# Casting the next panel's weights ahead of the head squares in the first unit of a query or key panel

## The reference: what is computed

```python
h = _rmsnorm(x, g_mix)
z = h @ w_in
u, va, q, k, v, gate_a, gate_b = jnp.split(z, cuts, axis=-1)
u = jax.nn.gelu(u)
va = _rmsnorm(jax.nn.gelu(va), g_v)
a = mix_a(u, va, w_s, b_s)
q = _rotary(_rmsnorm(q.reshape(*lead, N_HEADS_B, HEAD_DIM), g_q), pos)
k = _rotary(_rmsnorm(k.reshape(*lead, N_HEADS_B, HEAD_DIM), g_k), pos)
v = v.reshape(*lead, N_HEADS_B, HEAD_DIM)
b, kv_states = mix_b(q, k, v)
merged = jax.nn.sigmoid(gate_a) * (a @ w_oa) + jax.nn.sigmoid(gate_b) * (b @ w_ob)
x = x + merged @ w_o
```

## Time and profile before

| | us |
|---|---|
| Median of 3 runs | 1079.61 |
| Lowest, highest | 1078.57, 1081.40 |
| The profiled execution | 1077.97 |
| Its span, first to last instruction | 1076.3 |

### The profile page before, as it was taken

The page is one execution under the profiler, slowest core; times in us unless marked ns, Lnnn a source line. Parts: engine busy times, 40 slices in busy tenths (PEclk is TensorE's granted clock), DMA queues, the critical chain, the costliest instruction groups (busy, mean ns, idle before and its releaser), DMA issues.

```text
span 1076.3 us, 21532 instructions
## 1 busy us (share of the span) xinstructions
PE 1043.8 (97%) x8507; PEld 1030.8 (96%) x8508; DVE 690.3 (64%) x881; ACT 484.1 (45%) x1181; POOL 242.7 (23%) x374
## 2 busy tenths in 40 slices
PE   8999999999987999999999999999999999999996
PEld 8999999999987998999999999999999999999996
DVE  5579888988887778999583354344434443445552
ACT  6772888569634664352264543123312321333331
POOL 2441334014210014949101210010001000102300
PEclk9999999999998999999999999999999999999999
DMA  6557565776797564777732345555555555555512
GB/s 199 197 174 233 189 199 177 258 223 209 218 264 234 177 199 146 220 202 209 244 117 77 106 144 196 166 186 191 194 168 184 191 197 174 182 188 166 165 41 83
DMA packets 131090, 196.20 MB, mean 182 GB/s; under 512 B 32208, under 2 KB 108272, under 8 KB 129216
## 3 DMA queue, kind: packets, MB, share of 16 engines
q1 hardware_dynamic: 105808, 122.46, 35.9%
q0 software_dynamic: 10304, 63.28, 18.6%
q10 hardware_dynamic: 14896, 9.34, 2.9%
HBM read 186.07 MB, written 62.00 MB: 230 GB/s over the span
## 4 chain that ended last, share of the span: by engine, by line
PE 67%; DVE 13%; ACT 6%; issue 5%; DMA 4%; SPq 4%; ACTq 1%; POOL 0%; DVEq 0%; POOLq 0%
PE gm L1112 53%; PE gm L1088 3%; PE gm L1089 3%; PE gm L1090 3%; DMA w_raw<-in_w_in 2%; DVE w_lo L1391 2%; ACT prob L953 2%; DVE kv L1553 2%; DVE kv L1512 1%; DVE acc L1559 1%; SPq L587 1%; ACT sq L663 1%; SPq L539 1%; ACT w_hi L644 1%; ACTq L968 1%
## 5 line engine op out<-in xcount | busy, mean ns | idle before, releaser
L1112 PE MATMUL gm<-h_hi,w_hi 128*128 128x272 f32 x1088 | 227.8, 291 | 0.3 <-issue 0.3
L1112 PE MATMUL gm<-h_hi,w_lo 128*128 128x272 f32 x1088 | 225.1, 288 | 0.0
L1112 PE MATMUL gm<-h_lo,w_hi 128*128 128x272 f32 x1088 | 224.3, 288 | 0.0
L644 ACT CAST w_hi<-w_raw 128x1024 fp32r<-128x1024 f32 x150 | 150.5, 1044 | 157.9 <-PE gm L1112 116.5
L1391 DVE TENSOR_TENSOR w_lo<-w_raw,w_hi 128x1024 fp32r<-128x1024 f32 x150 | 178.2, 1227 | 40.2 <-ACT w_hi L644 38.0
L1088 PE MATMUL gm<-w_hi,h_hi 128*128 128x256 f32 x640 | 187.3, 293 | 4.6 <-issue 4.4
L1089 PE MATMUL gm<-w_hi,h_lo 128*128 128x256 f32 x640 | 181.1, 283 | 0.0
L1090 PE MATMUL gm<-w_lo,h_hi 128*128 128x256 f32 x640 | 180.3, 282 | 0.0
L1112 PEld LDWEIGHTS gm<-h_hi,w_hi 128*128 128x128 f32 x1088 | 170.5, 188 | 1.1 <-issue 0.5
L1112 PEld LDWEIGHTS gm<-h_lo,w_hi 128*128 128x128 f32 x1088 | 171.0, 189 | 0.0
L1112 PEld LDWEIGHTS gm<-h_hi,w_lo 128*128 128x128 f32 x1088 | 169.9, 189 | 0.0
(11 more groups left out here) (263 smaller groups left out, 1531.3 us busy)
## 6 DMA issues: line engine op xcount, KB each, us to landing
w_raw<-in_w_ff SPq DMA_DIRECT2D x64, 512.0 KB, 5.1
out_kvs<-in_cache_kv_w POOLq DMA_DIRECT2D x64, 510.0 KB, 4.3
w_raw<-in_w_in SPq DMA_DIRECT2D x60, 512.0 KB, 6.4
kv<-in_cache_kv_w SPq DMA_DIRECT2D x128, 128.0 KB
kv<-in_cache_kv_w SPq DMA_DIRECT2D x64, 256.0 KB
out_kvs<-in_cache_kv_w POOLq DMA_DIRECT2D x32, 508.0 KB, 4.8
kv<-in_cache_kv_w POOLq DMA_DIRECT2D x128, 64.0 KB, 3.5
w_raw<-in_w_o SPq DMA_DIRECT2D x8, 512.0 KB, 4.8
```

Of the source, the lines that this page charges most:

```text
L644: nc.scalar.copy(w_hi[:, r, hh * 1024:(hh + 1) * 1024], w_raw[:, hh]).then_inc(w_hi_done, 1)
L1112: last = nc.tensor.matmul(gm[:, 2 * b2 + half, 0:HALF], w, x[:, k0 + k, half * HALF:(half + 1) * HALF], start=first, stop=end)
```

## The change

For q, k and va panels, the two casts of the next panel's weights are issued inside `evacuate`, right behind the copy of the first unit, and therefore ahead of the squares of q and k. For v and oa panels they stay behind `evacuate`. The instructions and their waits are the same.

```diff
                         nc.scalar.copy(z[:, r, 0:n], src).then_inc(unit_out, 1)
+                        if sub == 0:
+                            split_hi(p + 1, (p + 1) % 2, panel_end(p - 1) if p >= 1 else None)
                         if kind != "va":
                             act.wait_ge(unit_out, u + 1)
                             square_heads(u, slice(0, 128), slice(0, 128), z[:, r], 8, r)
...
                 evacuate(s)
-                if late_split(s):
+                if late_split(s) and kind in ("v", "oa"):
                     split_hi(p + 1, (p + 1) % 2, panel_end(p - 1) if p >= 1 else None)
```

## The result

The changed kernel takes 1083.27 us (median of 11 runs, 1079.65 to 1086.11) against 1079.61 us (11 runs, 1075.88 to 1081.65) of the kernel before: ratio 1.0036, 95% interval 1.0022 to 1.0049. In microseconds that is 3.7, where the prediction had 2.8; the time predicted was 1082.4 us. The loss is real, and its middle lies just beyond the 0.3% that the prediction had set as its limit for no change. The profiled execution took 1083.2 us (span 1081.6 us), 5.2 us more than the one of before, which was itself a quick one. 0.54 us of that lie ahead of the start of panel 1 (31.79 against 31.25) and are not the change's: the granted clock of the first 16 us was 0.89 in it and 1.00 in before, and of all 14 executions traced the four with 0.89 there begin panel 1 0.54 to 0.75 us later, the others within 0.13 us of before.

What follows compares the result with a forecast made beforehand. TensorE, busy 97%, was taken as the bound; 0.4 us (panel 6) + 0.5 us (panel 9) + 1.93 us (panel 12) made 2.8 us, put on the median 1079.61 us: 1082.4 us, +0.26%, range 1078.0 to 1086.0 us.

Steps and rivals of the forecast that it cites:

- What bounds the kernel: TensorE, busy 97% of 1076.3 us; a change helps only by shortening its waits and hurts by making one longer.
- The earlier cast brings nothing: Panels 0 to 2: split weights end about 1 us earlier, but TensorE has no wait there; bounds 0 to 2.9 us, taken 0.
- Panel 12: Squares stand behind late weights, so 1.93 us falls on all that follows; TensorE's transposes near 227 wait 1.5 to 2 us.
- Panel 9: GpSimd's root falls into VectorE's subtractions and delays `scale_heads`: 0 to 0.95 us, taken 0.5 us.
- Panel 6: Squares wait for weights landing at about 109.7, exponential 0.75 us later; 0.4 us taken for the loop of ScalarE and VectorE.
- No link with slack over 0.3 us: From `scale_heads` at 233.79 to TensorE's wait ending at 339.27, lag on the loop reaches the end of the program.
- Behind 340 everything shifts alike: After the long wait ending at 339.27 the order is unchanged, so all later work moves by the same lag.
- slower by weights that land later: Rival, chance 0.30: panel 12's second half lands later than 224.6, moving squares and transposes equally; 1083.4 to 1085.4 us.
- Swallowed: Rival, chance 0.11: SyncE's queue sets the landing at 337.0, so TensorE's wait ending at 339.27 absorbs the loss; 1079.6 us.
- Faster: Rival, chance 0.12: earlier casts free `w_raw` earlier, shrinking VectorE's backlog and panel-start waits; 1077.1 us, or 1074.2 us.
- panel starts 7, 13, 15, 16 without a wait: Sign that the forecast is wrong: TensorE no longer idle at the starts of these panels.

Runs made afterwards that it cites:

- The table of four: Lag at panel 16, panel 12's order against its weights: old late 0, new late +2.28 us, new with weights early -0.97 us, old with weights early not run.
- the table of landings: Ten full-load kernels: panel 12's second-half landing against lag growth to panel 16; the new order adds 1.87 to 1.99 us to the landing.
- only 6: New order of casts and squares in panel 6 alone, against the kernel before: 1079.43 against 1080.41 us, ratio 0.9983.
- the change with loads ahead: Whole change, with four loads of V put behind panel 13's weights in SyncE's queue, against the kernel before: 1081.97 against 1079.71 us, ratio 1.0012.
- the change again: The changed kernel unaltered, timed once more against the kernel before: 1083.75 against 1079.71 us, ratio 1.0040.
- the six kernels of the table: Panel starts against before: the change, its repeat, and the new order in panel 12 alone, 6 alone, the other ten, and 6 and 12; +0.84 to +4.26 us at panel 16.
- both groups' loads ahead: Old order, loads of V of slots 35 and 53 both put behind the next load of weights, against the kernel before: 1082.54 against 1079.71 us, ratio 1.0025.
- the first run: Old order, four loads of V put behind panel 13's weights in SyncE's queue, against the kernel before: 1077.66 against 1079.71 us, ratio 0.9982.
- second run: Old order, four loads of V put behind panel 13's weights, timed again against the kernel before: 1077.97 against 1079.65 us, ratio 0.9985.

## Why the prediction was right, and where it was off

- **What bounds the kernel**: right. TensorE has the same 97%, and what was lost is waits of it at the places named.
- **The earlier cast brings nothing**: right. In panels 0 to 2 VectorE's wait for the cast is gone, and the panels start where they did. `scale_heads` waits 1.88 to 1.90 us for GpSimd there, and since the pair ahead of it ends earlier, it begins about 1.0 us later than in before, the upper end of the predicted 0 to 1 us. It is hidden, as forecast.
- **Panel 12**: right, in place, mechanism and size. 1.93 us were predicted, 2.03 and 2.04 us came with the whole change, 2.26 us alone; the difference between these lies in the landings. TensorE's wait at the transposes is 1.63 us (1.5 to 2 predicted), the start of panel 13 moves by 0.74 us (0.73 predicted), and the later `scale_heads`, 238.61 in after, still waits 2.45 us for GpSimd, no less than before. The table of four shows the cause by taking the late landing away, the table of landings by its size.
- **Panel 9**: right. 0.5 us were predicted; `scale_heads` waits 0.42 us, and the ten other panels alone move panel 12 by 0.36 us, 0.30 us of it between panels 10 and 12. The root takes 2.49 us. The Trainium skill (SBUF — State Buffer, section "Who interferes with whom") has a VectorE instruction with two SBUF inputs contend with a GpSimd instruction that reads SBUF; the roots of 2.48 and 2.49 us agree with it, and of the 0.95 us that it would give at panel 9, 0.3 to 0.5 us arrived.
- **Panel 6**: the term that was mis-sized. 0.4 us were put into the sum, 1.47 us came in after, and 0.37 to 2.0 us in five kernels with the new order. Two steps failed. The landing at 109.7 was taken as a constant from one trace; aligned at panel 1, it lies between 109.37 and 111.77 over the seven kernels with the old order and the full load there, and after's 111.70 lies within that spread, so the change did not make it late. And the loop was followed over the maxima only, as "of 0 to 0.75 us I take 0.4 us"; the root in VectorE's pair, charged to panel 9 alone, falls into panel 6 too once the squares end late enough. It delays `scale_heads` by 0.42 us in only 6, and by 1.56 us, with TensorE's transposes by 1.0 us, in after and in the change with loads ahead. Where the weights landed at 110.45, in the change again, the 0.4 us was met with 0.37 us.
- **Between panels 10 and 12** after has 0.76 us. The 0.30 us of panel 9's root are among them; panel 6 alone adds 0.28 us there, with panel 9 unchanged, and what hands that on was not looked for.
- **"No link with slack over 0.3 us"**: wrong as a statement, small in its effect up to the long wait. In before the first matmul of panel 18 already stood idle for 1.76 us (317.48), and in after it does not wait at all, so between the starts of panels 17 and 18 the lag falls from 6.36 to 4.60 us. What is given back there had come just before: ScalarE issues its moves of O from its own queue, and ahead of panel 17 four of them took 2.43 us of issuing in before and 4.10 us in after, so that the casts behind them came late, and with them panel 17 (the 1.93 us at 309.22 above). From panel 16 to the end of the long wait the lag changes by -0.5 to +0.4 us in the six kernels of the table, so what reached panel 16 did go on to there, as forecast. "Behind 340 everything shifts alike" did not hold: from the long wait to the end of the span the lag changes by -0.2 to +1.7 us in these six, and by +5.1 us with both groups' loads ahead. ScalarE in before, then in after:

```profile
292.12 2.43 ACTq L968 DMA_DIRECT2D O<-O_blk  x4
```

```profile
297.56 4.10 ACTq L970 DMA_DIRECT2D O<-O_blk  x4
```

- **Rivals**: "slower by weights that land later" is partly what happened, at panel 6 and hardly at panel 12, where the second half took 5.9 us and landed 0.16 us later than in before, against the panel's start. "Swallowed" is out: the wait before 339.27 is 5.92 us in after and was 6.19 us, so it took up 0.3 us of the lag. "Faster" is out: no panel of after starts earlier than in before. The waits at the starts of panels 7, 13 and 18 did shrink, from 0.89, 0.91 and 1.76 us to 0.17, 0 and 0 us, but TensorE had waited shortly ahead of them, 0.56 us at 116.11, 1.63 us at 231.69 and 1.93 us at 309.22. So "panel starts 7, 13, 15, 16 without a wait", named as a sign of being wrong, came true for panel 13 and was no such sign: the later transposes had taken the wait over. (The waits ahead of panels 15 and 16, read as about 0.3 and 0.4 us, have an idle time of 0.13 and 0.27 us in before, and 0.12 and 0.27 us in after.) A lower granted clock, which the prediction did not name, is out as well: over the timed runs of the repetition the mean granted clock is 0.992 with the change and 0.991 before, and the change is 4.0 us slower there.

**The sum by what was measured**: 1.5 (panel 6) + 0.8 (panels 10 and 11, with panel 9's root) + 2.0 (panel 12) = 4.3 us in the profiled execution, 3.2 us in the repeated one, against 2.8 us. The timed 3.7 us lies between. How near the forecast came is thus in part luck: one and the same kernel had 1.47 us and 0.37 us from panel 6.

What stays open: which transfers delay the weights of panels 6 and 12 from run to run, how panel 6 hands on 0.28 us behind panel 10, and how the changes of the lag behind the long wait divide between the clock and TensorE's waits.

## What to carry to other kernels

Before a step that waits for a transfer is put ahead of a step that doesn't, look at when the transfer lands in every iteration, not in the usual one: an engine works in order, so the independent work then starts when the transfer lands, and its engine loses at most the smaller of that wait and that work in each late iteration. Panel 12 paid all of it, 1.9 us; panel 6 paid 0.4 to 2.0 us, with what the later root added. Two late iterations of twelve made most of this loss, and the ten others gave nothing back. A landing time from one trace is a sample; give it a range as wide as similar loads show.

## What the runs showed of the hardware

Issuing a load earlier made it land little earlier: issued 4.6 and 6.4 us ahead, the two halves landed 1.0 and 0.5 us ahead in the first run and 1.5 us ahead, both, in the second. These are windows of the whole core, 211 to 215, 215 to 219 and 219 to 225 us, in before and then with the loads ahead (second run); ahead stand the length and the busy time of PE, PEld, DVE, ACT and POOL, and the three columns at the end are the granted clock, the DMA engines' busy share and GB/s.

```profile
211.00:215.00 4.00, 4.00 (x37) 4.00 (x36) 3.96 (x4) 1.22 (x3) 0.00 (x0) 1.00 0.93 283
215.00:219.00 4.00, 4.00 (x37) 4.00 (x35) 3.87 (x5) 0.27 (x1) 0.58 (x1) 1.00 0.66 183
219.00:225.00 6.00, 6.00 (x58) 5.75 (x57) 5.86 (x9) 4.03 (x19) 2.70 (x3) 1.00 0.80 241
```

```profile
211.00:215.00 4.00, 4.00 (x37) 4.00 (x36) 3.97 (x4) 1.22 (x3) 0.00 (x0) 1.00 0.94 289
215.00:219.00 4.00, 4.00 (x37) 4.00 (x36) 3.87 (x5) 0.27 (x1) 0.58 (x1) 1.00 0.94 247
219.00:225.00 6.00, 6.00 (x58) 5.75 (x57) 5.86 (x10) 5.12 (x22) 2.78 (x3) 1.00 0.67 187
```

The DMA engines' busy share was 0.93 already, without these loads, in the stretch in which they were issued ahead, and it is in the lull behind that it rises (0.66 to 0.94). Loads of 32 KB issued at the same time landed 7.2 and 7.0 us after it, not 9.6 to 12.0.

The wait of `scale_heads` for the root comes in steps. In panels 6 and 12 it is 0, 0.42 or 1.56 to 1.57 us, over the eight kernels with the new order in one of them, and nothing between. In panel 9 the root starts at 175.07, inside the first subtraction of the pair (174.81, half of 2.36 us), and ends 0.4 us behind the pair; in panels 6 and 12 it starts at 116.66 and 231.50, inside the second, and ends 1.5 us behind it. That fits a root that stands still until the subtraction under way is done and is not held by the next one; it was not tested by itself.
